# Router and state space products reordered in a fused encoder layer: last logits, token lists, first weight splits

## The reference, cut to what matters

```python
coarse = h @ w_coarse + b_coarse              # 4 groups
grp = top_k(coarse, 1); p_grp = softmax(coarse)[grp]
fine_g = (h @ w_fine + b_fine)[group grp]     # 4 experts in each group
top_v, top_i = top_k(fine_g, 2); w_top = softmax(top_v) * p_grp
comb = sum over both choices of one_hot(4 * grp + top_i) * w_top
for each expert e:  y += (silu(h @ w_gate[e]) * (h @ w_up[e]) * comb[:, e]) @ w_down[e]
out = RMSNorm(x + y)
```

## Time and profile before

| what | value |
|---|---|
| median of 3 runs | 661.93 us (661.85 to 664.66) |
| profiled execution, its own time | 661.45 us |
| its span | 659.5 us, 9075 instructions |
| TensorE matmul busy | 602.1 us (91%) |
| VectorE busy | 423.7 us (64%) |
| ScalarE busy | 325.1 us (49%) |
| GpSimd busy | 209.6 us (32%) |
| DMA | 110.40 MB, mean 167 GB/s |
| the chain that ended last | PE 72%, DVE 13%, DMA 6%, issue 4%, ACT 2% |

### The profile page before, as it was taken

How to read it: one execution, slowest core, us unless ns; L and a number is a source line. 1 busy time by engine, 2 the same in 40 slices (tenths; PEclk the granted TensorE clock), 3 DMA queues, 4 the chain that set the end, 5 groups by cost and what they waited for, 6 DMA issues and landing times.

```text
span 659.5 us, 9075 instructions
## 1 busy us (share of the span) xinstructions
PE 602.1 (91%) x3177; PEld 490.5 (74%) x3177; DVE 423.7 (64%) x784; ACT 325.1 (49%) x534; POOL 209.6 (32%) x219
## 2 busy tenths in 40 slices
PE   1998999998999999999999999999279999999990
PEld 1787898786977767777777888888258888888870
DVE  3989410389156755444752359452859999999966
ACT  4866332122235343454243435321348988989852
POOL 4418952398000180000000000012454454543920
PEclk9999997999999999999999999998579999999996
DMA  9993321221052232222222333984399999999364
GB/s 297 193 200 96 113 79 33 65 78 52 33 159 65 68 92 65 64 65 65 82 78 65 95 97 105 280 295 155 130 325 408 374 381 393 390 389 381 99 132 159
DMA packets 88608, 110.40 MB, mean 167 GB/s; under 512 B 19391, under 2 KB 66577, under 8 KB 88568
## 3 DMA queue, kind: packets, MB, share of 16 engines
q1 hardware_dynamic: 76952, 93.13, 42.9%
q0 software_dynamic: 6656, 14.05, 7.9%
q10 hardware_dynamic: 4960, 2.70, 1.5%
HBM read 102.08 MB, written 14.75 MB: 177 GB/s over the span
## 4 chain that ended last, share of the span: by engine, by line
PE 72%; DVE 13%; DMA 6%; issue 4%; ACT 2%; SPq 1%; ACTq 0%; POOL 0%; DVEq 0%; POOLq 0%
PE bank L1506 19%; PE bank L1508 18%; PE bank L1507 18%; DMA acc_scratch<-ysb,idx 4%; DVE w_lo L956 2%; PE bank L1681 2%; PE bank L1655 2%; PE bank L1668 2%; PE bank L1842 2%; PE bank L1581 1%; PE bank L1616 1%; PE bank L1792 1%; PE bank L1592 1%; DMA xf<-acc_scratch 1%; DVE e_lo L1420 1%
## 5 line engine op out<-in xcount | busy, mean ns | idle before, releaser
L956 DVE TENSOR_TENSOR w_lo<-raw,w_hi 128x1024 fp32r<-128x1024 f32 x55 | 72.0, 1311 | 119.5 <-ACT w_hi L559 119.1
L1506 PE MATMUL bank<-h_hi,w_hi 128*128 128x512 f32 x320 | 130.2, 407 | 1.6 <-DVE w_lo L956 1.6
L1508 PE MATMUL bank<-h_hi,w_lo 128*128 128x512 f32 x320 | 126.3, 395 | 0.0
L1507 PE MATMUL bank<-h_lo,w_hi 128*128 128x512 f32 x320 | 126.0, 394 | 0.0
L1420 DVE TENSOR_TENSOR e_lo<-eraw,e_hi 128x2048 fp32r<-128x2048 f32 x48 | 108.7, 2292 | 6.1 <-ACT e_hi L842 4.6
L842 ACT CAST e_hi<-eraw 128x2048 fp32r<-128x2048 f32 x48 | 91.9, 1919 | 7.5 <-PE bank L1508 5.9
L559 ACT CAST w_hi<-raw 128x1024 fp32r<-128x1024 f32 x55 | 57.7, 1048 | 31.5 <-PE bank L1508 31.5
L1506 PEld LDWEIGHTS bank<-h_hi,w_hi 128*128 128x128 f32 x320 | 61.3, 191 | 14.2 <-DVE w_lo L956 2.1
L1508 PEld LDWEIGHTS bank<-h_hi,w_lo 128*128 128x128 f32 x320 | 61.0, 191 | 13.4
L1507 PEld LDWEIGHTS bank<-h_lo,w_hi 128*128 128x128 f32 x320 | 61.3, 192 | 11.8
L2073 POOL TENSOR_TENSOR wcf<-wcf,prt 128x160 f32<-128x160 f32 x1 | 0.5, 456 | 194.8 <-DMA wcf<-in_moe_w_fine 194.8
(11 more groups left out here) (384 smaller groups left out, 1251.5 us busy)
## 6 DMA issues: line engine op xcount, KB each, us to landing
raw<-in_w_in SPq DMA_DIRECT2D x40, 512.0 KB, 3.8
eraw<-in_moe_w_gate SPq DMA_DIRECT2D x32, 512.0 KB, 6.9
eraw<-in_moe_w_up SPq DMA_DIRECT2D x32, 512.0 KB, 12.3
eraw<-in_moe_w_down SPq DMA_DIRECT2D x32, 512.0 KB
raw<-in_w_out SPq DMA_DIRECT2D x8, 512.0 KB, 3.7
x_sb<-in_x SPq DMA_DIRECT2D x4, 512.0 KB, 5.3
raw<-in_w_mem_kv SPq DMA_DIRECT2D x4, 512.0 KB, 6.9
raw<-in_w_br_na SPq DMA_DIRECT2D x4, 512.0 KB, 3.5
```

Source lines behind the costliest of these rows:

```text
L956: dve.tensor_tensor(v(l_, o, [1, 1024]), v(raw, 1024 * (c % RAW), [1, 1024]), raw32(v(h_, o, [1, 1024])), SUB).then_inc(sem("w_lo_done"), 1)
L1506: pe.matmul(dst, w[0], x[0], start=first, stop=False)
L1507: pe.matmul(dst, w[0], x[1], start=False, stop=False)
L1508: return pe.matmul(dst, w[1], x[0], start=False, stop=last)
```

## The change

On TensorE `s5_inputs` moves from behind chunk 13 into chunk 14, ahead of its third contraction step, and `s5_outputs` from behind chunk 19 into chunk 20, ahead of its sixth. ScalarE's `take_y` moves with it. The order of the last logits becomes turn 2, logits 1, turn 3, logits 2, logits 3; tile 3's logits get a bank of their own, so that VectorE scales tiles 0 to 2 before they are there. GpSimd multiplies tile 3 by the norm's weights ahead of ScalarE's scaling instead of behind it (the squares' unused output then goes to `gfin`). The one-hot becomes one instruction of 512 columns, the list two instead of three. Unit 0's split moves ahead of the router's end on ScalarE and behind the first list on VectorE; unit 1's behind the h2 scaling and behind `xt_rest(0)`; unit 2's ahead of the second expert's tokens. The first expert's product waits for the first half of `xt_lo` alone.

```diff
...
             if c in SLOTS:
                 slot(s)
                 s += 1
+            if c == C_S5G:
+                take_y()
             if c in SPLITS:
                 split_hi(*SPLITS[c])
             for kind, _ in tiles_of(c):
...
                 take_lags()
             if c == 12:
                 take_shifts()
-            if c == 19:
-                take_y()
             if c in (22, 23):
                 act.wait_ge(sem("gelu_in"), c - 21)
                 act.activation(v(glut, SEQ * (c - 22), [1, SEQ]), v(yT, SEQ * (c - 22), [1, SEQ]), ACT.Tanh,
...
         act.dma_start(v(wcf, 4, [20, KD], [1, 16]),
                       a["moe_w_fine"][0].rearrange("(k p) n -> p k n", p=P)).then_inc(sem("wcf_in"), 16)

+        def unit_hi(n, j, load, dst):
+            act.wait_ge(sem(f"e_in{j}"), 32 * load)
+            if not (isinstance(n, int) and n < 3):
+                act.wait_ge(sem("e_used"), n - 2)
+            act.copy(v(e_hi[dst], 0, [1, 2048]), v(eraw[j], 0, [1, 2048])).then_inc(sem("e_hi_done"), 1)
+
         def square_x2(n):

             act.wait_ge(sem("x2"), n + 1)
-            act.activation(v(h2, D * n, [1, D]), v(x_sb, D * n, [1, D]), ACT.Square,
+            junk = v(h2, D * n, [1, D]) if n < NT - 1 else v(gfin, 0, [1, D])
+            act.activation(junk, v(x_sb, D * n, [1, D]), ACT.Square,
                            accum_out=v(stat, n, [1, 1])).then_inc(sem("squares"), 1)

         def x2_take(n, j):
...
         square_x2(NT - 1)
         x2_take(NT - 1, 0)
         roots(NT + 3, NT - 1, 1)
+        unit_hi(0, 0, 1, 0)
         act.wait_ge(sem("last_root"), 1)
-        act.activation(v(h2, D * (NT - 1), [1, D]), v(x_sb, D * (NT - 1), [1, D]), ACT.Identity,
+        act.wait_ge(sem("h2_g"), 1)
+        act.activation(v(h2, D * (NT - 1), [1, D]), v(h2, D * (NT - 1), [1, D]), ACT.Identity,
                        scale=v(stat, 24 + NT - 1, [1, 1])).then_inc(sem("h2_scaled"), 1)
         act.dma_start(v(gfin, 0, [1, D]), a["final_norm"].partition_broadcast(P)).then_inc(sem("gf_in"), 16)
+        unit_hi(1, 1, 1, 1)

         act.wait_ge(sem("route_arg"), 1)
         act.activation(v(rt, 960, [1, 20]), v(rt, 960, [1, 20]), ACT.Exp).then_inc(sem("route_exp"), 1)

-
-        def unit_hi(n, j, load, dst):
-            act.wait_ge(sem(f"e_in{j}"), 32 * load)
-            if not (isinstance(n, int) and n < 3):
-                act.wait_ge(sem("e_used"), n - 2)
-            act.copy(v(e_hi[dst], 0, [1, 2048]), v(eraw[j], 0, [1, 2048])).then_inc(sem("e_hi_done"), 1)

         def xt_take(e, odd):
             if isinstance(e, int) and e == 1:
...
                 act.wait_ge(sem("at"), e)
                 act.copy(v(at_hi, 0, [1, 256]), pv(6, 0, [1, 256])).then_inc(sem("at_hi"), 1)
             if not peeled or e < 15:
+                if peeled and e == 0:
+                    unit_hi(2, 2, 1, 2)
                 xt_take(e + 1, 1 - odd)
-                unit_hi(3 * e + 2, n0 % EU, load_of(n0, i), 2)
+                if not peeled or e >= 1:
+                    unit_hi(3 * e + 2, n0 % EU, load_of(n0, i), 2)
             elif e == 15:
                 unit_hi(47, 47 % EU, load_of(47, 0), 2)
             if not peeled or e < 16:
...
                                          ACT.Identity, scale=v(wcur, 0 if odd else 1, [1, 1]))
                 ins.then_inc(sem("y_a"), 1)

-        unit_hi(0, 0, 1, 0)
-        unit_hi(1, 1, 1, 1)
         xt_take(0, 0)
         for e in range(3):
             step(e)
...

-        dve.wait_ge(sem("logits"), NT)
         dve.wait_ge(sem("lb_in"), 32)
         for n in range(NT):
-            ins = dve.scalar_tensor_tensor(v(rt, 20 * n, [1, 20]), pv(5, 20 * n, [1, 20]), v(stat, 24 + n, [1, 1]),
+            if n in (0, NT - 1):
+                dve.wait_ge(sem("logits"), NT if n else NT - 1)
+            ins = dve.scalar_tensor_tensor(v(rt, 20 * n, [1, 20]), pv(5 + n // 3, 20 * n, [1, 20]), v(stat, 24 + n, [1, 1]),
                                            v(lbias, 0, [1, 20]), MUL, ADD)
         link(ins)
         for j in range(4):
...

         def one_hot(e):

-            for n in range(NT):
-                ins = dve.tensor_scalar(v(hot, P * (NT * e + n), [1, P]), v(slots, P * e, [1, P]),
-                                        v(rt, 1020 + NHOT * n + e, [1, 1]), None, ALU.is_equal)
-            ins.then_inc(sem("hot"), 1)
+            dve.tensor_tensor(v(hot, P * NT * e, [P, NT], [1, P]), v(slots, P * e, [0, NT], [1, P]),
+                              v(rt, 1020 + e, [NHOT, NT], [0, P]), ALU.is_equal).then_inc(sem("hot"), 1)

         def slot_list(e):

             dve.wait_ge(sem("hot_used"), e + 1)
-            dve.tensor_copy(v(rt, 1056 + e, [1, 1]), pv(HOT_BANK[e], 0, [1, 1]))
-            link(dve.tensor_scalar(v(rt, 1060 + e, [1, 1]), pv(HOT_BANK[e], 1, [1, 1]), float(P), None, MUL))
-            dve.tensor_tensor(v(idx0, e, [1, 1]), v(rt, 1056 + e, [1, 1]), v(rt, 1060 + e, [1, 1]), ADD).then_inc(
-                sem("idx0"), 1)
+            link(dve.tensor_copy(v(rt, 1056 + e, [1, 1]), pv(HOT_BANK[e], 0, [1, 1])))
+            dve.scalar_tensor_tensor(v(idx0, e, [1, 1]), pv(HOT_BANK[e], 1, [1, 1]), float(P),
+                                     v(rt, 1056 + e, [1, 1]), MUL, ADD).then_inc(sem("idx0"), 1)
+
+        def unit_lo(n, j, dst):
+            dve.wait_ge(sem("e_hi_done"), n + 1)
+            dve.tensor_tensor(v(e_lo[dst], 0, [1, 2048]), v(eraw[j], 0, [1, 2048]),
+                              raw32(v(e_hi[dst], 0, [1, 2048])), SUB).then_inc(sem("e_lo_done"), 1)
+
+        def xt_rest(e, odd):
+            for j in range(2):
+                dve.wait_ge(sem("xt_hi"), 2 * e + j + 1)
+                dve.tensor_tensor(v(xt_lo[odd], 512 * j, [1, 512]), pv(4 + j, 0, [1, 512]),
+                                  raw32(v(xt_hi[odd], 512 * j, [1, 512])), SUB).then_inc(sem("xt_lo"), 1)

         one_hot(0)
         one_hot(1)
         slot_list(0)
+        unit_lo(0, 0, 0)
         one_hot(2)
         slot_list(1)
         one_hot(3)
...
         dve.tensor_tensor(raw32(v(pay, 9, [2, NT])), raw32(v(pay, 1, [2, NT])), v(rt, 976, [1, NT]), MUL).then_inc(sem("wts"), 1)

-        def unit_lo(n, j, dst):
-            dve.wait_ge(sem("e_hi_done"), n + 1)
-            dve.tensor_tensor(v(e_lo[dst], 0, [1, 2048]), v(eraw[j], 0, [1, 2048]),
-                              raw32(v(e_hi[dst], 0, [1, 2048])), SUB).then_inc(sem("e_lo_done"), 1)
-
-        def xt_rest(e, odd):
-            for j in range(2):
-                dve.wait_ge(sem("xt_hi"), 2 * e + j + 1)
-                dve.tensor_tensor(v(xt_lo[odd], 512 * j, [1, 512]), pv(4 + j, 0, [1, 512]),
-                                  raw32(v(xt_hi[odd], 512 * j, [1, 512])), SUB).then_inc(sem("xt_lo"), 1)
-
         def step(e0, i=None):

             peeled = i is None
...
                 dve.tensor_tensor(v(at_lo, 0, [1, 256]), pv(6, 0, [1, 256]), raw32(v(at_hi, 0, [1, 256])),
                                   SUB).then_inc(sem("at_lo"), 1)
             if not peeled or e < 15:
+                if peeled and e == 0:
+                    unit_lo(2, 2, 2)
                 xt_rest(e + 1, 1 - odd)
-                unit_lo(3 * e + 2, n0 % EU, 2)
+                if not peeled or e >= 1:
+                    unit_lo(3 * e + 2, n0 % EU, 2)
             if not peeled or e < 16:
                 b = 1 if odd else 0
                 dve.wait_ge(sem("tanh"), e + 1)
...
                                                  v(wcur, j, [1, 1]), raw32(v(y_parts[j], 512 * b, [1, 512])), MUL,
                                                  SUB).then_inc(sem("y_lo"), 1)

-        unit_lo(0, 0, 0)
+        xt_rest(0, 0)
         unit_lo(1, 1, 1)
-        xt_rest(0, 0)
         for e in range(3):
             step(e)
         with dve.Fori(0, 2) as i:
...
             for k in range(ks):
                 if SLOTS.get(c, 0) == 2 and k == 5:
                     slot(s)
+                if c == 14 and k == 2:
+                    s5_inputs()
+                if c == C_S5G and k == 5:
+                    s5_outputs()
                 if g == 0:
                     pe.wait_ge(sem("turn_lo"), k + 1)
                 ins = split(pv(g % 2, 0, [1, n]), [v(w, w0 + wk * k + wcol, [1, P]) for w in ws],
...
                 lags()
             if c == 12:
                 shifts()
-            if c == 13:
-                s5_inputs()
-            if c == 19:
-                s5_outputs()

         def out_part(n, c, first):
...
         def logits(n):
             pe.wait_ge(sem("x2_took"), 2 * n + 2)
             for k in range(KD):
-                ins = pe.matmul(pv(5, 20 * n, [1, 20]), v(x2T, SEQ * k + P * n, [1, P]), v(wcf, 20 * k, [1, 20]),
+                ins = pe.matmul(pv(5 + n // 3, 20 * n, [1, 20]), v(x2T, SEQ * k + P * n, [1, P]), v(wcf, 20 * k, [1, 20]),
                                 start=k == 0, stop=k == KD - 1)
             ins.then_inc(sem("logits"), 1)

...
         out_tile(3)
         x2_turn(2)
```

(14 more changed lines are left out.)

## The result

The changed kernel takes 654.85 us (median of 4 runs, 652.04 to 656.54), the kernel before 662.75 us beside it; the ratio is 0.9877, 95% interval 0.9842 to 0.9912. Predicted were 655.7 us, range 652.3 to 659.8, and "faster". Two more measurements of the same kernel gave 654.92 us (ratio 0.9883, 0.9853 to 0.9914) and 654.75 us (0.9895, 0.9874 to 0.9916).

A forecast was written before the change was run, and what follows sets the result against it. TensorE was taken as the bound before 200 us, a VectorE chain in the router. Front 4.3 plus 1.9 kept at the experts' start, 6.2 us off the profiled 661.45, gave 655.25, as a median 655.7 us; range 652.3 to 659.8.

The forecast's parts named there:

- Part 1: State space input products inside chunk 14: six matmuls cover TensorE's 1.0 us wait for upk, gain 1.0 us.
- Part 2 on TensorE: Output products inside chunk 20: the 3.0 us states wait filled, 1.85 us of clock kept, together 4.85 us.
- The cap by the y path: Store, 16 small loads and GELU argument limit the front to 4.3 us; VectorE then waits about 1.5 us.
- Router up to the first list: Logits, scaling, comparison and one-hots in the router: the first list comes 2.5 us earlier.
- the logits' term: Router: tile 2's 16 logit matmuls cover tile 3's copies, end 462.6 against 463.4, gain 0.8 us.
- Held gather: First gather after the list, held by a weight split: ends about 471.85 instead of 473.16, a lead of 1.3 us.
- Tickets: Slot scatters to wcur at the experts' start: third and fourth held, TensorE's 6 us lead shrinks to 1.9.
- tickets unharmed: Rival, 12%: at the experts' start descriptors slip between the splits, lead 4.9 us, 652.7 us.
- tickets take all: Rival, 25%: another scatter or gather is caught, ScalarE scales at 505 as before, 657.6 us.
- the front gives half: Rival, 15%: GELU wait costs the clock or states come later than 163.9; front 2.5 us, time 659 us.
- the move does nothing: Rival, 4%: in the front, TensorE's wait reappears at the state space wait inside chunk 20, 659 us.
- The slower one: Rival, 4%: the experts' scatters queue behind 2 to 3 MB more weight loads, tickets at 510, 666 us.

The follow-up runs named there:

- in_only: The kernel before with only the state space input products moved inside chunk 14; 662.16 us in a single execution, the kernel before 662.22 us.
- y_few: The changed kernel with five of the sixteen yT loads issued by GpSimd and eleven by SyncE; 653.31 us, ratio 0.9867 to the kernel before.
- after_again: The changed kernel unchanged, measured a second time beside the first experiments; 654.92 us, ratio 0.9883 to the kernel before.
- after_third: The changed kernel unchanged, measured a third time beside later experiments; 654.75 us, ratio 0.9895 to the kernel before.
- scale_late: The changed kernel with ScalarE's first output scaling put behind the next expert's casts and one weight split; 656.58 us, ratio 0.9919 to the kernel before.
- split0_yfew: The changed kernel with VectorE's first weight split after wcur and five of sixteen yT loads on GpSimd; 650.70 us, ratio 0.9831 to the kernel before.
- split2_late: The changed kernel with both halves of unit 2's split put back behind the first expert's tokens; 655.46 us, ratio 0.9892 to the kernel before.
- y_split: The changed kernel with the eight odd ones of sixteen yT loads issued by GpSimd; 652.89 us, ratio 0.9856 to the kernel before.

## Why the prediction was right

The time, the sign and the mechanisms came as forecast. Part of the closeness in time is luck: the gain was forecast at 6.2 us and the medians give 7.9, but the forecast started from 661.93, and the kernel before took 662.75 beside the changed one. The router's term was too small, the front's 4.3 us was close.

- **Part 1**, 1.0 predicted, 1.1 in the table. What was missing is the condition: alone it is worth 0 (`in_only`), as the states come no earlier with it once column 109 is taken off.
- **Part 2 on TensorE**, 4.85 predicted, 4.2 found. Wait and slow groups went as worked out (0.3 us of wait left, 1.16 for 0.95). The products began at 165.93, not 163.9; 1.6 us of those 2.0 are the longer slow stretch before 109.
- **The cap by the y path.** Predicted: a front of 4.3 us with VectorE waiting about 1.5 and TensorE 1.9 us. Found: 4.1 (from 1.6 to -2.5), 1.07 and 1.5. The working had the right link: the GELU argument starts 192.80 - 190.22 = 2.58 us earlier, TensorE's shift behind it is 2.6. The copy of `ypk` was forecast 1.8 us earlier and came 0.46 later, by the late products above; the last load lands at 190.2 all the same. `y_few` shows the cap by taking it away. The clock held in this execution; in `after_again` it did not, and 1.0 us went (-2.6 to -1.5), the risk that the prediction named; its front gave 3.0 us, that of `after_third` 3.9. The windows of `after_again`, then of the changed kernel:

```profile
196.00:200.00 4.00, 4.00 (x18) 3.19 (x15) 2.95 (x4) 1.48 (x3) 0.00 (x0) 0.57 0.29 92
```

```profile
196.00:200.00 4.00, 4.00 (x25) 3.26 (x22) 2.96 (x4) 1.47 (x3) 0.00 (x0) 1.00 0.32 93
```

- **Router up to the first list.** Predicted 2.5 us, found 3.4: the gather starts 472.04 - 466.14 = 5.90 us earlier, of which 2.5 are the front. Comparison (0.20) and one-hots (1.29 for two, 0.6 each predicted) are as priced. At the first comparison's start the lead is 4.62 - 2.5 = 2.1 us where the terms before it gave 1.3; the missing 0.8 is in the logits' term (0.8 predicted, 1.6 found): the last 32 records took 5.20 us, where 1.8, 0.4 and 3.6 had been added up.
- **Held gather.** As predicted, over 2 us (2.23). The first product starts 6.84 us earlier (474.56 for 481.40), less the front 4.3, where 3.25 were predicted.
- **Tickets.** The mechanism stood: third and fourth scatter held (3.09 and 1.90 us), ScalarE waiting 4.10 us for `wcur`, predicted "some 4". The step that failed in size is the start of the scatters: "0.45 us earlier", found 4.24 - 2.5 = 1.7 (first scatter at 472.69 for 476.93), 0.9 of it from the faster lists above. The last scatter so ended 0.4 us earlier against the front (485.71 for 488.65) where 0.8 later was predicted; its landing took 0.9 us longer, `wcur` came 2.32 - 2.5, or 0.2 us later, and the stage kept 2.9 us instead of 1.9. In `after_again` and `after_third`, with the better router clock, `wcur` came 1.8 us earlier against the front and 4.8 were kept, so 1.9 was low by 1.0 to 2.9 us. The Trainium skill's rule in "SBUF — State Buffer", section "SBUF: two separate sides", that VectorE with two SBUF inputs and a GpSimd operation that reads SBUF lock each other out for a whole instruction, agrees with the held rows here in one direction: 0.97 alone, 1.90 to 3.09 beside splits of 2.24, while the splits were not lengthened by the scatters (4.48 for two). The lead of 0 that it leaned to did not come: two scatters were held, as forecast, no third.
- **"The last experts and the closing chain move as a whole"** was true of this change, and has less room than it read: in `scale_late` the accumulating scatters took back 4.4 of 5.3 us there.
- **Sum.** 4.3 + 1.9 = 6.2 predicted; by the traces 4.1 + 2.9 = 7.0 against the shift ahead of the edits, in `after_again` 3.0 + 4.8 = 7.8, in `after_third` 3.9 + 4.8 = 8.7; the medians give 662.75 - 654.85 = 7.9, the three ratios 7.0 to 8.1.

Of the rivals, "tickets unharmed" fell (line 896 waits 4.1 us), as did "tickets take all" (2.9 us kept), "the front gives half" (4.1) and "the move does nothing". The slower one did not show: `idx` is read back 2.1 us earlier. That GpSimd waits 3.94 us for the scatters' landing where it was 5.08 does not mean a faster landing: the gather ahead of this wait was held for 3.05 us (1.05 before). From the last scatter's end to the readback it is 7.30 us, 6.44 before, far from the 5 us and more of that rival. Which of the removed waits would have mattered without part 2 was tried only for part 1.

## What to carry to other kernels

Filling one wait on an engine is worth only what the next path behind it lets through: follow the data from the moved work to its last reader and subtract, as the y path's 2.58 us did here. Where one engine runs long two-input operations while another issues small indirect transfers, place the long ones in the first engine's own idle time (0.5 to 1.0 us by the profiles for one moved split, more by the medians, 2.6 between `split0_yfew` and `y_few`, whose intervals overlap). It also pays to look for the one arrival behind which a whole stage follows at a fixed distance, as the last split follows 125.6 us behind the first use of `wcur`. And before moving loads to an idle queue, ask what the relieved queue will send next: the gain came only when its large loads could not overtake the small ones.

## What was not expected of the hardware

- A GpSimd operation and even a copy of one column are held by a VectorE split like a descriptor instruction is: `wcur` 2.32 us for two in `split2_late`, 0.31 in the changed kernel. In the kernel before it was VectorE that paid: 1.04 us for a 20-column comparison beside GpSimd's multiply, 0.20 without.
- Small loads that need 1.8 to 2.5 us to land took up to 5.2 when another queue began three loads of 512 KB, the first half a microsecond before the last of them (`y_split`).
- The same code ahead of every edit differed by up to 4.3 us between executions (column 109), mostly through the length of one stretch at the lower clock. A single profile does not tell a gain of 2 us. A difference between two columns of the same profile tells more, but not across the router, where the same kernel made 6.0, 7.3 and 7.5 us.
